# Block products: the prologue and the group steps in another order, and the probabilities scaled on ScalarE

## The chip, the cores and the metric

The kernel runs on one core of a Trainium2 chip. What counts is the device time of one execution in microseconds (us), the median over several runs. All tensors are 32-bit floats.

## The reference

Two decoder layers over 528 tokens (16 learned meta tokens ahead of 512), 1024 channels, inner width 2048. Layer 0 is gated linear attention with 4 heads, layer 1 forgetting attention with 16 heads of width 128. The change lies in layer 1:

```python
k, v, f_logit = split(rmsnorm(h, kv_norm_g) @ w_kv)            # keys and values of 16 heads, one forget logit a head
cum = cumsum(log_sigmoid(f_logit + b_forget))
q, r = split(rmsnorm(h, norm_g) @ w_in)                        # queries and gates
for start, end in blocks:                                      # 16 meta tokens, then blocks of 128
    s = q[start:end] @ k[:end].T * 128 ** -0.5 + cum[start:end, None] - cum[None, :end]
    p = softmax(where(causal, s, -1e30))
    outs.append(p @ v[:end])
h = h + (concat(outs) * silu(r)) @ w_out
out = rmsnorm(h, final_norm_g)[16:]
```

## The kernel before

Every float32 product is made of three: each operand is split into a high and a low half (a rounded copy by ScalarE, the difference by VectorE), and TensorE adds high times high, high times low and low times high (`project`, L1801). Activations lie with channels on the 128 partitions and tokens along the free dimension. Weights come in chunks of 128x1024 that SyncE loads into a ring of 6 (`raw`); ScalarE writes `w_hi` (ring of 4, L592), VectorE `w_lo` (ring of 6, L1085). The order of chunks is `CHUNKS` (L162), the order of TensorE's jobs `JOBS` (L129). Nothing is scheduled by a planner: each engine executes its own list in order, and semaphores tie them. `split_to(name)` makes all splits up to that chunk.

Layer 0 ends at 461 us. In the prologue of layer 1 TensorE makes the forget logits (`LOWF`), values of the meta tokens (m0), the keys k0, the values of the first four heads (u0, chunks u00 to u03, L2081) and the queries q0. Meanwhile VectorE takes the reciprocal root of the norm (L1104, 3.45 us), adds up the parts of the forget logits (L1588 to L1592), normalises in two halves (`norm`, L1576) and prepares keys and sums. `fox_values(0)` waits for the added logits (L2086), since its banks held their parts.

Then follows the loop over heads h (L1638 VectorE, L961 ScalarE, L2220 TensorE). Heads 2 to 11 (`strassen`, L99) make queries and gates together by seven block products on weights and on sums of tokens; their chunks are r, q and e, where e holds sums of weights made in place by VectorE (`weight_sums`, L1442). The sums of tokens (`t_raw`, `t_hi`, `t_lo`) are made once, around head 0. In such a step TensorE runs: scores of h, keys of h+1, first three products of h+1, transposes of the probabilities of h, middle three products, attention of h, last product. VectorE: maxima (L1533), low half of the first sum, the scaling of the probabilities (L1543), the keys with their norm (L1425), split of q, low keys, split of e, low probabilities, output sums. ScalarE: softmax (L896), gate by SiLU (L904), split of e, copy of the first product (L859), high keys (L842), high probabilities (L914). The scaling:

```python
nc.vector.reciprocal(inv[:, b:b + 1], tot[:, b:b + 1]).then_inc(inv_made, 1)
dve.wait_ge(inv_made, n)
v = pr[b][:, 0:KEYS[b]]
nc.vector.tensor_scalar(v, v, inv[:, b:b + 1], None, ALU.mult).then_inc(prob_scaled, 1)
```

for four blocks of 144, 272, 400 and 528 keys. Before the transposes TensorE waits for all four (L2136), before the middle products for the split of e (L2209), before the first products of head 2 for the gate of head 1 (L2199: `pe.wait_ge(fsilu_made, h)`). After heads 3, 7 and 11 stands a group step that makes the values of the next four heads (22.4 us of TensorE).

Of the kernel before, what the change touches and what calls it, by code (L numbers as in the profile page):

```python
# [11 lines left out]
P = 128  # L12
# [95 lines left out]
def fox_step(h):  # L108

    group = fox_group(h)  # L110
    jobs = [] if strassen(h) else [f"r{h}"]
# [8 lines left out]
def fox_chunks(h):  # L120
    group = fox_group(h)
    chunks = [] if strassen(h) else [f"r{h}"]
    if h + 1 < FOX_HEADS:
# [6 lines left out]
        + ["LOWF", "m0", "k0", "u0", "q0"] + [j for h in range(FOX_HEADS) for j in fox_step(h)] + [f"w{d}" for d in range(KT)])  # L130
# [4 lines left out]
for _job in JOBS:  # L135
# [19 lines left out]
    else:  # L155
# [7 lines left out]
          + ["k0", "u00", "u01", "u02", "u03", "q0"] + [x for h in range(FOX_HEADS) for x in fox_chunks(h)]  # L163
# [34 lines left out]
def program(nc, xT, consts, vecs, w_low, w_up, w_all, w_f, out, rows_out):  # L198
    with ExitStack() as c:
# [158 lines left out]
        def end_groups(g):  # L358
            if g in (0, NBLK - 1):
                return [y[0:META, (12 if g else 8) + n, 0:VH * P] for n in range(4)]  # L360
            return [ends[0:META, n // 2, n % 2 * VH * P:(n % 2 + 1) * VH * P] for n in range(4)]
# [123 lines left out]
        def _(sp):  # L485
# [37 lines left out]
            spread.update({CHUNK[f"k{h}"] + LO_RING: h for h in range(1, FOX_HEADS)})  # L523
# [55 lines left out]
        def _(act):  # L579
# [323 lines left out]

            def fox_gate(h):  # L904
# [9 lines left out]
            def probs_hi(h):  # L914
# [3 lines left out]
                if h // VH in (1, 2) and h % VH == 0:  # L918
                    act.wait_ge(end_lo, h // VH + 1)
# [34 lines left out]
            split_to("u03")  # L954
            end_values_hi(0)
            split_to("q0")
            split_to("r0")
            split_to("k1")
            fox_values_hi(0)
            queries_hi(0)  # L960
            for h in range(H):  # L961
                g = fox_group(h)
                if h + 1 < H and strassen(h + 1):
                    n = h + 1
                    split_to(f"r{n}")
                    if n == S0 or fox_group(h - 1) is not None:
                        sum_hi_first(n)
                    split_to(f"q{n}")
                    softmax(h)
                    fox_gate(h)  # L970
# [11 lines left out]
                    else:  # L982
# [7 lines left out]
                        split_to(f"r{n + 1}")  # L990
                        fox_values_hi(g)
                    continue
                if strassen(h):
                    split_to(f"q{h + 1}")
                else:
# [3 lines left out]
                softmax(h)  # L999
                if g is not None:  # L1000
                    split_to(f"u{g}0")
                elif h + 1 < H:
# [9 lines left out]
                if h == 0:  # L1012
                    for n in range(4):
                        act.wait_ge(t_made, 4)
                        nc.scalar.activation(t_hi[:, n], t_raw[:, n], ACT.Copy).then_inc(thi_made, 1)
# [5 lines left out]
                if h + 1 < H:  # L1021
# [3 lines left out]
                    else:  # L1025
                        split_to(CHUNKS[CHUNK[f"q{h + 1}"] + AHEAD])
                    queries_hi(h + 1)
                if g is not None:
# [48 lines left out]
        def _(dve):  # L1077
# [334 lines left out]
            nc.vector.memset(a_hi[0:R_ALL, AF_AT[NBLK]:AF_ALL].bitcast(F32), 0.0).then_inc(stack_zeroed, 1)  # L1412
# [988 lines left out]
```

## Time and profile before

| | us |
|---|---|
| median of 3 runs | 1028.55 (1028.09 to 1029.09) |
| the profiled execution | 1027.92, its span 1026.1 |
| TensorE busy | 1004.5 (98%) |
| VectorE busy | 692.1 (67%) |
| ScalarE busy | 534.2 (52%) |
| granted TensorE clock, mean | 0.993 |

In the views below PE is TensorE, PEld its weight loads, DVE VectorE, ACT ScalarE, POOL GpSimd, SPq the queue of SyncE. L1085 is line 1085 of the kernel. Times of a timeline are us from the start of the span, groups carry their mean in ns. What stands in brackets or behind the bar is the idle time before an instruction and what ended it. Matmuls overlap, so a start is the surer number.

### The profile page before, as it was taken

How to read it: one execution, taken by the hardware profiler on the slowest of the kernel's cores; microseconds unless marked ns; L12 is line 12 of the kernel's file. 1: busy time of each engine (PE TensorE's matmuls, PEld its weight loads, DVE VectorE, ACT ScalarE, POOL GpSimd, SP SyncE). 2: the span in 40 equal slices, each digit the busy share in tenths (PEclk: the TensorE clock that was granted, in tenths of full speed). 3: DMA queues.
4: the chain of work that ended last, by engine and by line, in shares of the span. 5: the costliest groups of instructions: out<-in, count | busy, mean ns of one | idle time of the engine just before them, and what ended most of it. 6: DMA issues, size and time to landing. Idle time of an engine off the chain costs nothing.

```text
span 1026.1 us, 18711 instructions
## 1 busy us (share of the span) xinstructions
PE 1004.5 (98%) x7627; PEld 937.6 (91%) x7627; DVE 692.1 (67%) x1142; ACT 534.2 (52%) x894; POOL 40.4 (4%) x69
## 2 busy tenths in 40 slices
PE   9999999999999999997989999999999999999998
PEld 8999999999999999995779988999899888888887
DVE  6875666677567783437779975898499846576333
ACT  6754644653483653335554654656366626464332
POOL 0000000000000000000201000100000100000000
PEclk9999999999999999998989999999999999999999
DMA  8211221121121123331323441443234553333412
GB/s 286 84 63 63 83 84 63 63 83 64 65 100 63 63 88 109 124 114 43 117 70 100 120 141 52 130 107 133 95 105 104 162 183 111 101 90 97 152 59 83
DMA packets 39798, 102.93 MB, mean 100 GB/s; under 512 B 4496, under 2 KB 12560, under 8 KB 39712
## 3 DMA queue, kind: packets, MB, share of 16 engines
q1 hardware_dynamic: 38992, 101.06, 32.1%
q8 instruction: 60, 0.98, 0.4%
q10 hardware_dynamic: 720, 0.68, 0.2%
q14 instruction: 26, 0.21, 0.1%
HBM read 94.41 MB, written 7.11 MB: 99 GB/s over the span
## 4 chain that ended last, share of the span: by engine, by line
PE 95%; DVE 2%; ACT 1%; DMA 0%; issue 0%; SPq 0%; DVEq 0%; ACTq 0%
PE psum L1808 60%; PE psum L2182 10%; PE psum L2102 9%; PE psum L2160 3%; PE psum L1933 2%; PE psum L2141 2%; PE psum L1881 1%; PE psum L2128 1%; PE psum L2129 1%; PE psum L2130 1%; PE psum L1929 1%; PE psum L1902 1%; PE psum L2067 1%; PE psum L1861 1%; DVE w_lo L1085 0%; DMA hT<-xT 0%
## 5 line engine op out<-in xcount | busy, mean ns | idle before, releaser
L1085 DVE TENSOR_TENSOR w_lo<-raw,w_hi 128x1024 fp32r<-128x1024 f32 x153 | 185.3, 1223 | 36.8 <-ACT w_hi L592 29.0
L592 ACT ACTIVATE w_hi<-raw 128x1024 fp32r<-128x1024 f32 x153 | 159.5, 1052 | 20.4 <-PE psum L2102 16.3
L1808 PE MATMUL psum<-xh,w_hi 128*128 128x264 f32 x768 | 159.1, 288 | 1.0 <-DVE w_lo L1099 0.8
L1808 PE MATMUL psum<-xl,w_hi 128*128 128x264 f32 x768 | 155.9, 285 | 0.0
L1808 PE MATMUL psum<-xh,w_lo 128*128 128x264 f32 x768 | 155.2, 283 | 0.0
L1808 PEld LDWEIGHTS psum<-xh,w_hi 128*128 128x128 f32 x768 | 118.5, 189 | 2.4 <-DVE xl L1114 1.4
L1808 PEld LDWEIGHTS psum<-xl,w_hi 128*128 128x128 f32 x768 | 119.5, 188 | 0.0
L1808 PEld LDWEIGHTS psum<-xh,w_lo 128*128 128x128 f32 x768 | 119.1, 189 | 0.0
L1808 PE MATMUL psum<-y_lo,w_hi 128*128 128x264 f32 (+2 forms) x400 | 104.8, 314 | 0.0
L571 POOL TENSOR_TENSOR sub<-sub,cst 128x128 f32<-128x128 f32 x64 | 38.7, 607 | 873.1 <-DMA sub<-sums 873.1
L1808 PEld LDWEIGHTS psum<-y_lo,w_hi 128*128 128x128 f32 x400 | 66.7, 188 | 4.6
L1099 DVE TENSOR_TENSOR hT<-psum,hT 128x528 f32<-128x528 f32 (+2 forms) x17 | 11.3, 667 | 71.1 <-PE psum L1808 71.1
L2102 PE MATMUL psum<-w_hi,zh 128*128 128x512 f32 x128 | 51.8, 405 | 6.0 <-DVE y L1099 6.0
L902 ACT ACTIVATE pr<-pr,top 128x144 f32<-128x144 f32 (+1 forms) x64 | 36.6, 573 | 32.7 <-DVE top L1531 32.7
L1808 PE MATMUL psum<-zh,w_hi 128*128 128x264 f32 x256 | 52.4, 286 | 0.8 <-DVE w_lo L1085 0.8
L1808 PE MATMUL psum<-z_hi,w_hi 128*128 128x512 f32 (+1 forms) x144 | 53.1, 369 | 0.0
L1808 PE MATMUL psum<-z_hi,w_lo 128*128 128x512 f32 (+1 forms) x144 | 52.8, 367 | 0.0
L1808 PE MATMUL psum<-y_hi,w_hi 128*128 128x264 f32 x256 | 52.0, 284 | 0.0
L1808 PE MATMUL psum<-zl,w_hi 128*128 128x264 f32 x256 | 51.9, 285 | 0.0
L1808 PE MATMUL psum<-y_hi,w_lo 128*128 128x264 f32 x256 | 51.8, 284 | 0.0
L1808 PE MATMUL psum<-zh,w_lo 128*128 128x264 f32 x256 | 51.8, 283 | 0.0
L2102 PE MATMUL psum<-w_lo,zh 128*128 128x512 f32 x128 | 51.2, 400 | 0.0
(322 smaller groups left out, 2347.0 us busy)
## 6 DMA issues: line engine op xcount, KB each, us to landing
raw<-w_all SPq DMA_DIRECT2D x143, 512.0 KB, 3.4
sub<-sums SPq DMA_DIRECT2D x16, 264.0 KB, 7.6
sub<-sums SPq DMA_DIRECT2D x16, 200.0 KB, 6.5
y_keep<-sq SPq DMA_DIRECT2D x11, 256.0 KB, 2.2
y<-y_keep SPq DMA_DIRECT2D x11, 256.0 KB, 4.0
sub<-sums SPq DMA_DIRECT2D x16, 136.0 KB, 5.0
hT<-xT SPq DMA_DIRECT2D x8, 264.0 KB, 5.4
h_keep<-hT SPq DMA_DIRECT2D x8, 256.0 KB, 4.1
```

The source lines that it names most:

```text
L571: nc.gpsimd.tensor_tensor(diag, diag, above, ALU.add).then_inc(sub_made, 1)
L592: nc.scalar.activation(w_hi[:, n % HI_RING, :], raw[:, n % LO_RING, :], ACT.Copy).then_inc(hi_made, 1)
L902: nc.scalar.activation(v, v, ACT.Exp, scale=-1.0, bias=top[:, b:b + 1], accum_out=tot[:, b:b + 1]).then_inc(prob_made, 1)
L1085: nc.vector.tensor_tensor(w_lo[:, n % LO_RING, :], raw[:, n % LO_RING, :], w_hi[:, n % HI_RING, :].bitcast(F32), ALU.subtract).then_inc(lo ...
L1099: nc.vector.tensor_tensor(out, a, b, op).then_inc(made, 1)
L1808: i = nc.tensor.matmul(o, w[a][:, k % KT, :], x[b][:, k, c0:c1], start=k == first and a == b == 0, stop=k == last and a == 1)
L1861: i = nc.tensor.transpose(bank(x + 1, b * P, (b + 1) * P), src[:, b * P:(b + 1) * P], ident)
L1933: nc.tensor.matmul(bank(x + 1, 400 - w, 400), vs[a][:, j, :], gs[b][:, A_DIAG[j]:A_DIAG[j] + w], start=False, stop=False)
L2102: i = nc.tensor.matmul(bank(4 + b), xk[a][:, k, b * BLK:(b + 1) * BLK], w[p][:, k % 2, :], start=k == a == p == 0, stop=k == KT - 1 and a ...
L2141: nc.tensor.transpose(bank(bk, c0, c0 + BLK), pr[b][:, BLK * j:BLK * j + BLK], ident)
L2160: nc.tensor.matmul(bank(slot(job), PT_Q0[j], SEQ), vs[a][:, j, v], ps[b][:, AF_AT[j]:AF_AT[j] + w], start=j == 0 and a == b == 0, stop=False)
L2182: i = nc.tensor.matmul(o, w[a][:, k0 + k, :], x[b][:, k, :], start=k == a == b == 0, stop=k == KT // 2 - 1 and a == 1)
```

## The change

The multiplies of the probabilities by their inverse sums go from VectorE to ScalarE, between the exponentials and the gate, in all 16 heads; VectorE keeps the reciprocals. In the prologue the forget logits are added ahead of the reciprocal root, the splits u01, u02 and u03 and the normalisations interleave otherwise, k1 is made right after u0, the token sums are made before head 0, and head 0 makes q1 and r1 so that head 1 makes only k2. In the group steps before heads 5 and 9 (of the block products) the split of r, both halves of the first sum and the split of q stand ahead of the value copies.

```diff
--- before.py
+++ after.py
@@ -108,7 +108,9 @@
 def fox_step(h):
 
     group = fox_group(h)
-    jobs = [] if strassen(h) else [f"r{h}"]
+    if h == 0:
+        return ["r0", "q1", "r1", "a0"]
+    jobs = [] if h <= 1 or strassen(h) else [f"r{h}"]
     if h + 1 == FOX_HEADS:
         return jobs + [f"a{h}"]
...
@@ -160,7 +164,7 @@
     _last[_area] = _job
 
 CHUNKS = ([c for h in range(GLA_HEADS) for c in gla_strips(h)] + [f"W{d}{half}" for d in range(KT) for half in "ab"]
-          + ["k0", "u00", "u01", "u02", "u03", "q0"] + [x for h in range(FOX_HEADS) for x in fox_chunks(h)]
+          + ["k0", "u00", "u01", "u02", "u03", "k1", "q0"] + [x for h in range(FOX_HEADS) for x in fox_chunks(h)]
           + [f"w{d}{half}" for d in range(KT) for half in "ab"])
 CHUNK = {c: n for n, c in enumerate(CHUNKS)}
...
@@ -901,6 +905,12 @@
                     v = pr[b][:, 0:KEYS[b]]
                     nc.scalar.activation(v, v, ACT.Exp, scale=-1.0, bias=top[:, b:b + 1], accum_out=tot[:, b:b + 1]).then_inc(prob_made, 1)
 
+            def scale_probs(h):
+                for b in range(NBLK):
+                    act.wait_ge(inv_made, NBLK * h + b + 1)
+                    v = pr[b][:, 0:KEYS[b]]
+                    nc.scalar.activation(v, v, ACT.Copy, scale=inv[:, b:b + 1]).then_inc(prob_scaled, 1)
+
...
@@ -951,22 +961,25 @@
             nc.scalar.activation(f_t, f_t, ACT.Ln, bias=1.0).then_inc(f_act, 1)
             act.wait_ge(x2_normed, 2)
             nc.scalar.activation(x2h[:, 4:8, :], x2n[:, 4:8, :], ACT.Copy).then_inc(x2h_made, 1)
-            split_to("u03")
+            split_to("k1")
             end_values_hi(0)
-            split_to("q0")
             split_to("r0")
-            split_to("k1")
             fox_values_hi(0)
+            split_to("q1")
             queries_hi(0)
+            act.wait_ge(t_made, 4)
+            for n in range(4):
+                nc.scalar.activation(t_hi[:, n], t_raw[:, n], ACT.Copy).then_inc(thi_made, 1)
...
                 if h + 1 < H and strassen(h + 1):
                     n = h + 1
                     split_to(f"r{n}")
-                    if n == S0 or fox_group(h - 1) is not None:
+                    if n == S0:
                         sum_hi_first(n)
                     split_to(f"q{n}")
                     softmax(h)
+                    scale_probs(h)
                     fox_gate(h)
...
@@ -988,17 +1001,24 @@
                         split_to(f"u{g}3")
                         split_to(f"k{n + 1}")
                         split_to(f"r{n + 1}")
+                        sum_hi_first(n + 1)
+                        split_to(f"q{n + 1}")
                         fox_values_hi(g)
...
+                elif h == 0:
+                    split_to("r1")
...
                 softmax(h)
+                scale_probs(h)
                 if g is not None:
                     split_to(f"u{g}0")
+                elif h == 0:
+                    split_to("k2")
                 elif h + 1 < H:
...
-                if h == 0:
-                    for n in range(4):
-                        act.wait_ge(t_made, 4)
-                        nc.scalar.activation(t_hi[:, n], t_raw[:, n], ACT.Copy).then_inc(thi_made, 1)
...
+                    if h == 0:
+                        split_to("r2")
...
@@ -1410,6 +1428,13 @@
             U_ORDER = (3, 2, 0, 1)
             nc.vector.memset(fv_end[0:R_ALL, :].bitcast(F32), 0.0).then_inc(stack_zeroed, 1)
             nc.vector.memset(a_hi[0:R_ALL, AF_AT[NBLK]:AF_ALL].bitcast(F32), 0.0).then_inc(stack_zeroed, 1)
+            x = slot("LOWF")
+            dve.wait_ge(f_copied, 1)
+            tt(two(fb), halves(x, H), two(f_a), ALU.add, f_sum)
+            for n, part in enumerate((f_t, f_u)):
+                dve.wait_ge(f_copied, n + 2)
+                dve.wait_ge(f_sum, n + 1)
+                tt(fb, fb, part, ALU.add, f_sum)
             done(dve, "m0")
             split_to("u00")
             inverse("x2", rstd[:])
...
@@ -1540,16 +1565,13 @@
                 maximum(h, 2)
                 maximum(h, 3)
 
-            def scale_probs(h):
+            def probs_inverse(h):
                 for b in range(NBLK):
                     n = NBLK * h + b + 1
                     dve.wait_ge(prob_made, n)
                     if h:
                         dve.wait_ge(prob_scaled, NBLK * h)
                     nc.vector.reciprocal(inv[:, b:b + 1], tot[:, b:b + 1]).then_inc(inv_made, 1)
-                    dve.wait_ge(inv_made, n)
-                    v = pr[b][:, 0:KEYS[b]]
-                    nc.vector.tensor_scalar(v, v, inv[:, b:b + 1], None, ALU.mult).then_inc(prob_scaled, 1)
 
             def probs_lo(h):
...
+            def token_sums_lo(n):
+                dve.wait_ge(thi_made, n + 1)
+                tt(t_lo[:, n], t_raw[:, n], t_hi[:, n].bitcast(F32), ALU.subtract, tlo_made)
+
...
-            x = slot("LOWF")
-            dve.wait_ge(f_copied, 1)
-            tt(two(fb), halves(x, H), two(f_a), ALU.add, f_sum)
-            for n, part in enumerate((f_t, f_u)):
-                dve.wait_ge(f_copied, n + 2)
-                dve.wait_ge(f_sum, n + 1)
-                tt(fb, fb, part, ALU.add, f_sum)
+            split_to("u01")
             dve.wait_ge(f_sum, 3)
             tt(fb, fb, rstd[0:H, :], ALU.mult, f_logit)
+            fox_key(0)
             norm(0)
-            split_to("u01")
             dve.wait_ge(f_logit, 1)
             dve.wait_ge(f_act, 1)
             nc.vector.tensor_scalar(fb, fb, vec[0:H, B_F:B_F + 1], 0.0, ALU.add, ALU.min).then_inc(f_min, 1)
+            split_to("u02")
             norm(1)
-            keys_lo(0)
-            for b in range(NBLK - 1):
-                nc.vector.memset(pr[b][:, KEYS[b]:PR_W[b]], 0.0).then_inc(pads, 1)
             dve.wait_ge(f_act, 3)
             dve.wait_ge(f_min, 1)
             tt(f_t, fb, f_t, ALU.subtract, f_log)
             dve.wait_ge(f_log, 1)
             nc.vector.tensor_tensor_scan(fb, ones[0:H, 0:1].to_broadcast([H, T]), f_t, 0.0, ALU.mult, ALU.add).then_inc(f_cum, 1)
+            split_to("u03")
             x = slot("m0") + 1
             dve.wait_ge(rtok_done, 1)
             nc.vector.tensor_copy(rtok[:, 0:NBLK], bank(x, ROOT_AT, ROOT_AT + NBLK * 32).rearrange("p (b n) -> p b n", n=32)[:, :, 0]).then_inc(rtok_made, 1)
             nc.vector.tensor_copy(rtok[0:META, NBLK:NBLK + 1], bank(x, ROOT_AT + 128, ROOT_AT + 129, 0, META)).then_inc(rtok_made, 1)
-            split_to("u02")
+            split_to("k1")
             norm_lo(0)
             end_values_sum(0)
+            norm_lo(1)
+            split_to("q0")
+            keys_lo(0)
+            for b in range(NBLK - 1):
+                nc.vector.memset(pr[b][:, KEYS[b]:PR_W[b]], 0.0).then_inc(pads, 1)
             dve.wait_ge(cum_done, 1)
             nc.vector.tensor_copy(cum_t[:].rearrange("p b h -> p (b h)"), bank(x, CUM_AT, CUM_AT + NBLK * H)).then_inc(cum_made, 1)
-            split_to("u03")
-            norm_lo(1)
             dve.wait_ge(rtok_made, 4)
             end_values_lo(0)
-            split_to("q0")
+            fox_values_lo(0)
             split_to("r0")
-            fox_values_lo(0)
+            token_sums(False)
             queries_lo(0)
...
+            token_sums(True)
+            split_to("q1")
...
@@ -1644,12 +1669,11 @@
                         split_to(f"r{n}")
                     maxima(h)
                     split_to(f"r{n}")
-                    sum_lo_first(n)
+                    if n == S0 or fox_group(h - 1) is None:
+                        sum_lo_first(n)
                     if h + 1 == S0:
-                        for i in range(4):
-                            dve.wait_ge(thi_made, i + 1)
-                            tt(t_lo[:, i], t_raw[:, i], t_hi[:, i].bitcast(F32), ALU.subtract, tlo_made)
-                    scale_probs(h)
+                        token_sums_lo(3)
+                    probs_inverse(h)
                     fox_key(n)
                     split_to(f"q{n}")
                     keys_lo(n)
@@ -1675,6 +1699,9 @@
                         split_to(f"u{g}3")
                         weight_sums(h + 2)
                         split_to(f"k{n + 1}")
+                        split_to(f"r{n + 1}")
+                        sum_lo_first(n + 1)
+                        split_to(f"q{n + 1}")
                         fox_values_lo(g)
                     continue
...
+                elif h == 0:
+                    split_to("r1")
...
-                scale_probs(h)
+                probs_inverse(h)
...
+                    if h == 0:
+                        split_to("k2")
+                    elif g is None:
                         split_to(CHUNKS[CHUNK[f"k{h + 1}"] + AHEAD])
                     fox_key(h + 1)
                     keys_lo(h + 1)
+                    if h == 0:
+                        for i in range(3):
+                            token_sums_lo(i)
...
-                    if g == 0 and part == 2:
+                    if g == 0 and part == 3:
                         sums_by_token()
...
             fox_values(0)
+            strip("k1", xk)
             pe.wait_ge(x2l_made, 2)
             strip_late("q0", xq)
...
+                elif h == 1:
+                    fox_scores(1)
+                    strip("k2", xk)
...
-                    if h + 1 < H:
+                    if h == 0:
+                        strip_late("q1", xq)
+                    elif h + 1 < H:
                         strip(f"k{h + 1}", xk)
...
                 if h + 1 < H:
-                    strip_late(f"q{h + 1}", xq)
+                    strip_late(f"q{h + 1}" if h else "r1", xq)
```

## Rows read from the trace of the kernel before

**Rows 1.** The page, busy time of each engine: us, share of the span, instructions.
```profile
PE 1004.5 (98%) x7627; PEld 937.6 (91%) x7627; DVE 692.1 (67%) x1142; ACT 534.2 (52%) x894; POOL 40.4 (4%) x69
```

**Rows 2.** TensorE's waits: who waited for whom, us in total, times, longest.
```profile
PE psum L2102 <- DVE y L1099: 6.0, 1, 6.0
PE psum L2128 <- DVE sq L1099: 5.1, 1, 5.1
PE psum L2182 <- DVE w_lo L1085: 2.6, 2, 1.3
PE psum L1808 <- DVE w_lo L1085: 0.8, 1, 0.8
```

**Rows 3.** Stretches: busy us by engine, then granted clock, DMA share, GB/s.
```profile
474.00:476.00 2.00, 2.00 (x6) 1.57 (x5) 2.00 (x2) 0.49 (x1) 0.00 (x0) 0.50 0.00 0
...
534.00:536.00 2.00, 2.00 (x8) 2.00 (x9) 1.93 (x4) 1.44 (x2) 0.00 (x0) 0.50 0.35 131
...
642.00:644.00 2.00, 0.95 (x10) 0.66 (x8) 1.76 (x3) 2.00 (x4) 0.67 (x2) 1.00 0.77 144
```

**Rows 4.** Timeline of VectorE, 466 to 475: start us, us, operation, idle before.
```profile
466.15 3.45 DVE L1104 RECIPROCAL rstd<-sq 128x528 f32<-128x528 f32 x1
...
471.04 1.50 DVE L1099 TENSOR_TENSOR y<-y 16x528 f32<-16x528 f32 x2
...
473.20 2.27 DVE L1099 TENSOR_TENSOR y<-x2g,rstd 128x2048 f32<-128x2048 f32 x1
```

**Rows 5.** Timeline of VectorE, head 1: weight sums, low halves of t, reciprocal.
```profile
533.70 0.68 DVE L1452 TENSOR_TENSOR s_raw<-raw 128x512 f32<-128x512 f32 x1
...
541.63 4.62 DVE L1099 TENSOR_TENSOR y_lo<-y,y_lo 128x1024 fp32r<-128x1024 f32 x4
...
546.18 0.16 DVE L1549 RECIPROCAL inv<-tot 128x1 f32<-128x1 f32 x1
```

**Rows 6.** ScalarE's groups, 540 to 930: busy us, mean ns, idle before.
```profile
L902 ACT ACTIVATE pr<-pr,top 128x528 f32<-128x528 f32 x15 | 10.8, 722 | 0.0
...
L902 ACT ACTIVATE pr<-pr,top 128x400 f32<-128x400 f32 x15 | 9.5, 630 | 8.0 <-DVE top L1531 8.0
...
L902 ACT ACTIVATE pr<-pr,top 128x272 f32<-128x272 f32 x14 | 7.3, 524 | 5.2 <-DVE top L1531 5.2
...
L894 ACT ACTIVATE fv_hi<-psum,rtok 128x512 fp32r<-128x512 f32 x12 | 7.3, 690 | 30.2 <-PE psum L2102 30.2
...
L902 ACT ACTIVATE pr<-pr,top 128x144 f32<-128x144 f32 x14 | 5.8, 416 | 17.6 <-DVE top L1531 17.6
...
L852 ACT ACTIVATE fq_hi<-psum 128x512 fp32r<-128x512 f32 x4 | 2.4, 598 | 9.7 <-PE psum L1808 9.7
```

**Rows 7.** Timeline of ScalarE, head 5, 659 to 664.
```profile
659.33 0.72 ACT L902 ACTIVATE pr<-pr,top 128x528 f32<-128x528 f32 x1
659.96 0.19 ACT L902 ACTIVATION_READ_ACCUMULATOR pr<-pr,top 128x1 f32 x1
660.16 1.28 ACT L907 ACT_TABLE_LOAD   x1
...
663.21 0.63 ACT L846 ACTIVATE fk_hi<-acc 128x528 fp32r<-128x528 f32 x1
```

**Rows 8.** Timeline of VectorE, head 5, 661 to 666.
```profile
661.39 0.49 DVE L1552 TENSOR_SCALAR pr<-pr,inv 128x528 f32<-128x528 f32 x1
...
663.87 0.71 DVE L1099 TENSOR_TENSOR fk_lo<-acc,fk_hi 128x528 fp32r<-128x528 f32 x1 [0.24 <-ACT fk_hi L846]
664.50 1.22 DVE L1085 TENSOR_TENSOR w_lo<-raw,w_hi 128x1024 fp32r<-128x1024 f32 x1
```

**Rows 9.** Chain that ended last, 600 to 680: start us, us, what.
```profile
644.24 4.58 PE psum L2182 x36
...
654.35 5.84 PE psum L1808 x48
```

**Rows 10.** Timeline of TensorE: first middle product of head 6.
```profile
665.85 0.50 PE L2182 MATMUL psum<-y_lo,w_hi 128*128 128x256 f32 x2
```

## What the change will do to the time

> **What bounds the kernel now.** I read the page's table of engines first: TensorE is busy 98% of the span, so what counts is where it stands still and where its clock is down [rows 1]. Then its own waits: 6.0 us before the first group of values, 0.8 us for a weight split in the second strip, 5.1 us before the scores of head 1, and 1.3 us in each of the two heads that follow a group step [rows 2]. After each of the two long waits the granted clock is at 0.50, the 1.2 GHz level, after the 1.3 us wait it stays at 1.00 [rows 3]. All the rest of the span TensorE runs without a gap. So an edit can win at most those waits with their slow stretches, about 18 us, and it can lose wherever another engine delivers only just in time. The place to look for that is the step of a block-product head (2 to 11), in the timelines of ScalarE and VectorE.
>
> There the row to see is the last split of a step. VectorE writes the low half of chunk e from 664.50 to 665.72 [rows 8], and TensorE starts the products that read it at 665.85 [rows 10]: some 0.1 us of slack. In front of it VectorE had idled 0.24 us for the high half of the keys [rows 8], which ScalarE makes as the last link of exponentials, table load, SiLU, split of e, copy, keys: the last exponential is read out at 660.15, the keys start at 663.21 [rows 7]. So ScalarE's chain sets the split of e, and the split of e sets TensorE. The pattern is the same in seven steps (heads 2, 3, 5, 6, 7, 9, 10, slack 0.05 to 0.15 us); in heads 4 and 8 it is already late by 1.3 us, the row of 644.24 being the late start [rows 9].
>
> **Part 1: the multiply on ScalarE, in all 16 heads.** VectorE loses four multiplies a head, ScalarE gains four Copies with a per-partition scale, placed between the last exponential and the table load for SiLU. No trace row shows that operation on these tiles. Nearest are the exponentials of the same four shapes, in place, with one per-partition operand: 416, 524, 630 and 722 ns [rows 6]. Consecutive ones overlap by some 0.1 us (the 528-wide one starts at 659.33 and its follower at 659.96, 0.63 us for 0.72) [rows 7], so the four hold the engine 2.29 - 0.4 = 1.9 us. Low bound: a 512-wide Copy with a scale takes 690 ns, one without 598 [rows 6]; were the operand free, 1.9 - 0.37 = 1.5 us. High bound: 2.1 us if each also pays some 0.05 us for its wait. I take 1.9, since both nearest rows with an operand agree. The four reciprocals that VectorE makes are ready before ScalarE needs the last, so they add nothing.
>
> What is queued behind: table load, SiLU, split of e, copy and keys on ScalarE all go 1.9 us later, VectorE's low keys and its split of e behind them, and TensorE waits 1.9 - 0.1 = 1.8 us more in each of the seven steps: 12.6 us. VectorE's freed time (some 1.3 us) buys nothing, since it lies behind the exponentials and becomes a wait for the keys. Nor is it caught up: VectorE's chain of a step starts at the end of the fourth product on TensorE, which moves along, so each step pays again.
>
> **Part 2: group steps.** Moving the split of r, the first sum's halves and the split of q of heads 5 and 9 ahead of the value copies takes about 2.9 us from VectorE's chain in heads 4 and 8 and 1.6 us from ScalarE's. These run in idle time there. The maxima can then follow the scores at once: last maximum about 636.5, exponentials about 637.5, scaled at 639.4, and then the 3.7 us from exponential to finished keys as in [rows 7], 0.6 and 1.2 us on VectorE [rows 8]: split of e ready near 645.0 against 644.2 today. So the gain is used up and each costs 0.7 us: 1.4 us. From head 11 on the multiplies finish early or the strip of keys covers them: nothing.
>
> **Part 3: the prologue.** Today the first values wait for three 16-row additions that stand behind a reciprocal of 3.45 us [rows 4]. With the additions ahead of it (two take 1.50 [rows 4]) the sum is ready near 466.3, the split of u00 ends near 467.5, and TensorE idles 0.9 us for 6.0, with no slow stretch. The old losses up to the first product are 6.0 + 2.0 (slow clock) + 0.8 + 5.1 + 1.9 (slow clock) = 15.8 us. Walking the new order with the durations of the old one, 2.27 for a normalisation half [rows 4], 1.2 for a split [rows 8], 5.84 for a strip of keys [rows 9], 1.28 for a table load [rows 7], I get new gaps. u02 now follows the table of f: +0.8. u03 and the root copies follow the second normalisation, which waits behind u02: +1.4. ScalarE's four t copies (3.9) now precede the softmax of head 0, and the scaled copies end 1.0 after the strip of q1. The strip of r1 reuses the bank of r0 and waits for SiLU of r0, which stands behind scaling, a split and a table load: +1.3. Three low halves of t (1.15 each, from 4.62 for four [rows 5]) stand ahead of the low probabilities: +1.3 before the attention of head 0. The scores of head 1 have no r1 part in front of them any more: +0.8.
>
> The largest is in head 1. The first product waits for SiLU of head 1 (its bank was r1's). Let X be the end of head 0's output. VectorE does weight sums, maxima, split, one low sum, one low half of t, first reciprocal: today 533.70 to 546.18, 12.5 us with four low halves [rows 5], so 9.0 with one, plus 0.1. Then ScalarE scales (1.9 + 0.1), loads the table (1.3), does SiLU (0.6) [rows 6, 7]: X + 13.0. TensorE has only scores (1.9) and the strip k2 (5.84): X + 7.7. That is a gap of 5.3 us, as long as the one it replaces, and I expect the clock to fall as it did there [rows 3]: +1.9. New losses: 0.9 + 0.8 + 1.4 + 1.0 + 1.3 + 1.3 + 0.8 + 5.3 + 1.9 = 14.7. Against 15.8 the prologue wins 1.1 us. Loads: SP's order moves k1 ahead of q0 and r0 and the sums of head 1 one slot back, to behind the maxima of head 0 and some 15 us ahead of their reader; I cost it at nothing, and if a load came late it would be one DMA of about 3.4 us.
>
> **Sum.** +12.6 + 1.4 - 1.1 = +12.9 us on the profiled execution's 1027.9 us (span 1026.1), 1040.8; the median of the runs is 0.6 above that execution, within the error. I take 1040.5.
>
> **Rivals.** (a) *The copies are hidden.* If keys and split of e had room the multiply would cost nothing, VectorE, the busier of the two, would be relieved, the 2.6 us in heads 4 and 8 would go, and the prologue would win up to 9 if the head-1 gap did not open: 1028 - 2.6 - 1.1 to - 9 = 1016 to 1024. For it: VectorE is busy some 18.5 of 20 us in these steps, ScalarE 12.5. Against it: the slack of 0.1 us and the 0.24 us wait for ScalarE [rows 8]. Chance 0.12. (b) *The clock falls at the repeated waits.* Nine waits of 1.8 to 2.0 us are longer than the 1.3 us after which it stayed up and shorter than the 5.1 us after which it fell [rows 3]. If it fell each time, at the 1.9 us taken above: 1040.5 + 9 x 1.9 = 1057.6. Chance 0.05. The Trainium skill, TensorE: Matmul & The Clock Gate, section on HAM oscillation, says that frequent short idles between groups of matmuls can let the clock swing; by that rule this case is the one to expect, and this trace shows the swing only after the two long waits. (c) *The costs and gains cancel*: scaling at 1.5 us (7 x 1.4 + 2 x 0.3 = 10.4) and a prologue that wins its full 9 us, 1029.5. Chance 0.03. Forecast (ScalarE's chain becomes the bound): 0.80.
>
> **How the numbers follow.** Own range of the forecast: low, 10.4 from scaling less up to 8 from the prologue, 1030.5; high, scaling at 2.1 (7 x 2.0 + 2 x 0.9 = 15.8) with a prologue that loses 2, 1045.7, and one or two falls of the clock, 1047. It leaves out (a), most of (b) and (c), about 0.2 in all, so 1030 to 1047 is also the range. A measurement of this kernel can tell about 0.2%, 2 us, from no change. Faster: (a), 0.12, and 0.01 of the forecast's low edge. Same: (c), 0.03. Slower: 0.84.
>
> **What would show it.** Right: TensorE waits of about 1.8 us before the middle products in seven heads and about 2.0 in heads 4 and 8, with VectorE waiting some 3.4 us for the high keys each time (0.24 + 1.9 + 1.3); the first wait of 6.0 down to about 1; a gap of some 5 us before the first product of head 2, released by SiLU. Part 1 is wrong if TensorE has no gap there, that is if the table load starts within 0.3 us of the last exponential or the keys start less than 3.5 us after it. Part 3 is wrong if the first product of head 2 starts earlier than 542 or later than 546.

## The result, and the profile of the changed kernel

The changed kernel takes 1047.38 us (median of 4 runs, 1043.55 to 1048.93); the kernel before, beside it, 1028.82 us (4 runs, 1028.09 to 1029.56). The ratio is 1.0175, 95% interval 1.0144 to 1.0205. The execution that was profiled took 1043.55 us with a span of 1041.7 us, the shortest of the four, 3.8 us under the median; why the runs differ by 5 us is a finding of its own below.

First the page of the changed kernel: span, and busy time of each engine with its share and its instructions.

```profile
span 1041.7 us, 18711 instructions
...
PE 1005.9 (97%) x7627; PEld 938.8 (90%) x7627; DVE 669.9 (64%) x1078; ACT 563.3 (54%) x958; POOL 41.4 (4%) x69
```

Against [rows 1], VectorE has 64 instructions and 22 us less, ScalarE 64 more and 29 us more, TensorE the same 7627 products. The busier helper was relieved and the kernel became longer, so the averages do not tell what happened. TensorE's waits do (who waited for whom, us in total, times, longest us), in the changed kernel:

```profile
PE psum L2215 <- DVE w_lo L1103: 18.2, 9, 2.4
PE psum L2215 <- ACT sq L922: 5.0, 1, 5.0
PE psum L1840 <- ACT sq L922: 1.2, 1, 1.2
PE psum L2134 <- DVE w_lo L1103: 1.1, 2, 0.9
PE psum L2109 <- DVE rtok L1643: 1.1, 1, 1.1
...
PE psum L2174 <- ACT pr L912: 1.0, 1, 1.0
PE psum L2193 <- DVE a_lo L1117: 0.9, 1, 0.9
PE psum L2161 <- DVE sq L1117: 0.9, 1, 0.9
```

The line number moved: L2215 is L2182 of before, and L1103 is L1085. The first row is the middle products of a step waiting for the split of e: 2 waits and 2.6 us in [rows 2], now 9 waits and 18.2 us. The second is the first product of head 2 waiting for SiLU of head 1, which was not there. The 6.0 and 5.1 us of [rows 2] are gone; the waits of about 1 us that took their place are the other rows.

The step of head 5 on ScalarE, where [rows 7] stood (start us, us, operation, shapes):

```profile
664.44 0.72 ACT L906 ACTIVATE pr<-pr,top 128x528 f32<-128x528 f32 x1
665.07 0.18 ACT L906 ACTIVATION_READ_ACCUMULATOR pr<-pr,top 128x1 f32 x1
665.16 1.96 ACT L912 ACTIVATE pr<-pr,inv 128x144 f32<-128x144 f32 x4
667.14 1.28 ACT L917 ACT_TABLE_LOAD   x1
...
670.19 0.63 ACT L850 ACTIVATE fk_hi<-acc 128x528 fp32r<-128x528 f32 x1
```

The four copies stand between the readout of the last exponential (665.07) and the table load (667.14). They hold the engine for 1.98 us, and the keys start 5.12 us after that readout begins where in [rows 7] they started 3.25 us after it. VectorE in the same step, with the idle time before an instruction and its releaser in brackets:

```profile
664.91 0.55 DVE L1574 RECIPROCAL inv<-tot 128x1 f32<-128x1 f32 x4
665.50 0.71 DVE L1450 SCALAR_TENSOR_TENSOR acc<-psum,rstd 128x528 f32<-128x528 f32 x1
...
670.85 0.92 DVE L1117 TENSOR_TENSOR fk_lo<-acc,fk_hi 128x528 fp32r<-128x528 f32 x1 [3.51 <-ACT fk_hi L850]
671.69 1.21 DVE L1103 TENSOR_TENSOR w_lo<-raw,w_hi 128x1024 fp32r<-128x1024 f32 x1
```

The time that VectorE gained stands in the brackets: 0.24 us of idle before the low keys in [rows 8], 3.51 us now. The split of e ends at 672.90, and TensorE starts the products that read it 0.06 us later, after a wait of 1.93 us:

```profile
672.96 0.51 PE L2215 MATMUL psum<-y_lo,w_hi 128*128 128x256 f32 x2 [1.93 <-DVE w_lo L1103]
```

Read one after another, the three views give the chain from a ScalarE copy to a TensorE wait, which the page's busy shares hide.

### The profile page after: what moved, and what is told of

It reads as the page before. It is cut to its first block, busy times and chain, and to the rows that moved or that the text cites. A ratio compares the mean times of both kernels' runs of the same rounds, so it can differ in the third digit from the quotient of the medians.

```text
span 1041.7 us, 18711 instructions
## 1 busy us (share of the span) xinstructions
PE 1005.9 (97%) x7627; PEld 938.8 (90%) x7627; DVE 669.9 (64%) x1078; ACT 563.3 (54%) x958; POOL 41.4 (4%) x69
## 4 chain that ended last, share of the span: by engine, by line
PE 79%; DVE 9%; ACT 7%; issue 4%; DMA 0%; DVEq 0%; ACTq 0%
PE psum L1840 54%; PE psum L2134 7%; PE psum L2215 6%; PE psum L1965 2%; PE psum L2193 2%; DVE w_lo L1103 2%; ACT pr L906 1%; PE psum L1913 1%; ACT pr L912 1%; ACT w_hi L596 1%; DVE pr L1549 1%; PE psum L1961 1%; ACT L917 1%; PE psum L2174 1%; PE psum L1934 1%
## 5 line engine op out<-in xcount | busy, mean ns | idle before, releaser
L1103 DVE TENSOR_TENSOR w_lo<-raw,w_hi 128x1024 fp32r<-128x1024 f32 x153 | 185.9, 1226 | 51.0 <-ACT w_hi L596 48.5
L1840 PEld LDWEIGHTS psum<-y_lo,w_hi 128*128 128x128 f32 x400 | 66.7, 188 | 4.6
L2215 PE MATMUL psum<-y_lo,w_hi 128*128 128x256 f32 x240 | 46.0, 293 | 18.2 <-DVE w_lo L1103 18.2
L1117 DVE TENSOR_TENSOR hT<-psum,hT 128x528 f32<-128x528 f32 (+2 forms) x17 | 11.3, 667 | 70.7 <-PE psum L1840 70.7
L2215 PEld LDWEIGHTS psum<-y_lo,w_hi 128*128 128x128 f32 x240 | 38.5, 198 | 19.4 <-DVE w_lo L1103 19.4
```

What stands on the lines that cost most here:

```text
L1103: nc.vector.tensor_tensor(w_lo[:, n % LO_RING, :], raw[:, n % LO_RING, :], w_hi[:, n % HI_RING, :].bitcast(F32), ALU.subtract).then_inc(lo ...
L1117: nc.vector.tensor_tensor(out, a, b, op).then_inc(made, 1)
L1840: i = nc.tensor.matmul(o, w[a][:, k % KT, :], x[b][:, k, c0:c1], start=k == first and a == b == 0, stop=k == last and a == 1)
L2215: i = nc.tensor.matmul(o, w[a][:, k0 + k, :], x[b][:, k, :], start=k == a == b == 0, stop=k == KT // 2 - 1 and a == 1)
```

## The experiments

All kernels compute everything. L numbers in a profile row are those of that kernel. Two theories were to be told apart. Theory A is the forecast: ScalarE's chain of exponentials, copies, table load, SiLU, split of e and keys sets TensorE in the steps, and the new order as such gains a little. Its rival B: the new order (or the extra work of the prologue) is what costs, and the copies are mostly hidden.

### One part alone, from both sides

The changed kernel with the multiplies back on VectorE (both calls of `scale_probs` go):

```
-                    scale_probs(h)
...
     nc.vector.reciprocal(inv[:, b:b + 1], tot[:, b:b + 1]).then_inc(inv_made, 1)
+    dve.wait_ge(inv_made, n)
+    v = pr[b][:, 0:KEYS[b]]
+    nc.vector.tensor_scalar(v, v, inv[:, b:b + 1], None, ALU.mult).then_inc(prob_scaled, 1)
```

> The changed kernel with the four multiplies a head back on VectorE, behind each reciprocal as in the kernel before; the new order stays. Theory (ScalarE's chain is what costs): no wait of TensorE before the middle products of the seven ordinary heads, about 0.1 us in heads 4 and 8 (1.3 before, 2.4 after); the gap before head 2's first product shrinks from 5.0 to about 1.4 us with no fall of the clock. 1027.9 - 8.9 (prologue) - 2.4 = about 1017 us. Rival (the new order costs a part of the loss): TensorE waits remain in the steps and the time is 1035 us or more.

Measured: 1017.75 us (1017.47 to 1017.95), ratio 0.9889, interval 0.9874 to 0.9903. Its TensorE waits:

```profile
PE psum L2216 <- DVE w_lo L1101: 1.3, 3, 0.6
PE psum L2194 <- DVE a_lo L1115: 1.2, 1, 1.2
...
PE psum L2216 <- ACT sq L922: 0.9, 1, 0.9
```

The new order alone wins 11.4 us. The nine waits of 18.2 us are three of 1.3 us, and the head-1 gap of 5.0 us is 0.9 us. So the copies also made the head-1 gap, and B falls: it needed a kernel that stays slow without them.

The other half, the multiplies on ScalarE in the order of before (the reverse of the diff above, in the kernel before):

```
                     softmax(h)
+                    scale_probs(h)
                     fox_gate(h)
...
-    nc.vector.tensor_scalar(v, v, inv[:, b:b + 1], None, ALU.mult).then_inc(prob_scaled, 1)
```

> The kernel before with nothing changed but the multiplies on ScalarE, between softmax and gate. Theory: seven waits of 1.8 us, 3.2 us in heads 4 and 8 (1.3 + 1.9), some 2.5 us new before head 2's first product: 1027.9 + 12.6 + 3.8 + 2.5 = about 1047 us, more if the clock falls at the new waits. Rival (the loss is the order's): within 3 us of the kernel before.

Measured: 1057.71 us (1055.94 to 1058.9), ratio 1.0281, interval 1.0264 to 1.0298, some 11 us above what was expected without falls of the clock. Its TensorE waits, then stretches of 2 us behind four of them (us from, us to, length, busy us of PE, PEld, DVE, ACT and POOL, granted clock, DMA share, GB/s):

```profile
PE psum L2187 <- DVE w_lo L1093: 22.2, 10, 3.4
PE psum L2107 <- DVE y L1107: 6.0, 1, 6.0
PE psum L2133 <- DVE sq L1107: 5.5, 1, 5.5
```

```profile
605.00:607.00 2.00, 1.75 (x8) 1.75 (x9) 1.94 (x5) 2.00 (x3) 0.45 (x1) 0.50 0.53 217
656.00:658.00 2.00, 1.95 (x9) 1.95 (x10) 1.90 (x4) 0.72 (x3) 0.31 (x1) 0.55 0.05 10
779.00:781.00 2.00, 2.00 (x12) 2.00 (x11) 1.73 (x5) 0.00 (x0) 0.00 (x0) 0.52 0.02 8
803.00:805.00 2.00, 2.00 (x10) 2.00 (x11) 1.71 (x4) 0.59 (x2) 0.58 (x2) 0.50 0.53 216
```

By the ratios the copies cost 28.9 us in the order of before and 29.4 us in the new one (1.0175 over 0.9889): the same within the intervals. In the order of before the waits explain some 20 us of it. The rest is the second thing to see here: behind four step waits of 1.7 to 3.4 us (heads 3, 4, 8 and 9) the granted clock is at 0.50 to 0.55, the 1.2 GHz level. The sum of 1 minus the granted clock over stretches of 1 us, called the lost clock below, is 14.6 us in this kernel and 7.0 us in the one before; each of the four falls has 1.7 us of it.

### How much slack the chain has

A small dose: 0.6 us of idle copies on ScalarE, into unused memory, in the same place of the kernel before.

```
                     softmax(h)
+                    for v in (spare[:, 0:106], spare[:, 106:212], spare2[:, 0:106]):
+                        nc.scalar.activation(v, reset[:, 0:106], ACT.Copy)
                     fox_gate(h)
```

> The kernel before with three idle copies of 106 columns on ScalarE between softmax and gate of heads 1 to 10, into unused memory, some 0.6 us. Theory (0.1 us of slack, each us on ScalarE there is a us of TensorE): waits of 0.5 us in seven heads and 1.9 in heads 4 and 8: 1027.9 + 3.5 + 1.2 = about 1032.6. Rival (ScalarE has room, only moving the multiplies as such costs): no change, 1028.

Measured: 1034.83 us (1034.76 to 1034.95), ratio 1.0055, interval 1.004 to 1.007. The waits for the split of e:

```profile
PE psum L2184 <- DVE w_lo L1087: 6.5, 9, 1.8
```

By time these are 0.48, 0.39, 1.82, 0.40, 0.39, 0.40, 1.83, 0.39 and 0.40 us in heads 2 to 10. The idle copies put off the table load of head 5 by 0.54 us: it starts 0.74 us behind the start of the last readout (662.98), where in [rows 7] it starts 0.20 us behind it.

```profile
662.98 0.19 ACT L902 ACTIVATION_READ_ACCUMULATOR pr<-pr,top 128x1 f32 x1
...
663.72 1.28 ACT L907 ACT_TABLE_LOAD   x1
```

So work that only takes ScalarE's time, with nothing of the probabilities in it, comes out on TensorE less some 0.1 us in six of the seven steps (0.54 to 0.4), and whole in heads 4 and 8, from 1.3 to 1.8. The slack of 0.1 us that the forecast read from [rows 8, 10] is thus shown. Behind both 1.8 us waits the clock fell (granted 0.72 and 0.73 in the 2 us behind), 1.7 us of lost clock each; the fall of head 1, ahead of them, is 1.7 us where the kernel before has 3.4. The lost clock is 8.8 us against 7.0, and these 1.8 us are most of the 2.2 us by which the run is above the expectation.

### Taking the link out

If it is the chain, its table load and SiLU can be moved out of it while the copies stay. In the changed kernel, the gate of heads 2 to 10 behind the high halves of the probabilities:

```
                     scale_probs(h)
-                    fox_gate(h)
+                    if h < S0:
+                        fox_gate(h)
                     split_to(f"e{n}")
...
                     probs_hi(h)
+                    if h >= S0:
+                        fox_gate(h)
```

> The changed kernel with the gate (table load and SiLU, 1.9 us) of heads 2 to 10 moved behind the high probabilities on ScalarE; the multiplies stay there. Theory (a serial chain exponentials, copies, gate, split of e, keys): the chain is as long as in the kernel before again, the seven waits vanish (-13), those of heads 4 and 8 fall to about 0.1 (-4.6), with them the fall of the clock in head 2 (-1.8): about 1024 us. The prologue keeps its 5 us gap. Rival (ScalarE is too busy, or the copies slow something else): the waits stay and the time is 1040 or more.

Measured: 1025.31 us (1024.9 to 1025.52), ratio 0.9962, interval 0.9947 to 0.9977. Its TensorE waits, and ScalarE in head 5:

```profile
PE psum L2218 <- ACT sq L922: 5.0, 1, 5.0
...
PE psum L2218 <- DVE w_lo L1106: 0.7, 2, 0.4
```

```profile
657.83 1.97 ACT L912 ACTIVATE pr<-pr,inv 128x144 f32<-128x144 f32 x4
659.70 1.04 ACT L596 ACTIVATE w_hi<-raw 128x1024 fp32r<-128x1024 f32 x1
...
665.64 1.28 ACT L917 ACT_TABLE_LOAD   x1
666.94 0.63 ACT L917 ACTIVATE sq<-sq 128x512 f32<-128x512 f32 x1
668.80 0.63 ACT L861 ACTIVATE fq_hi<-acc 128x512 fp32r<-128x512 f32 x1 [1.23 <-DVE acc L1120]
```

The 1.9 us of load and SiLU took the place that the copies had filled, seven waits are gone and the two of heads 4 and 8 are 0.41 and 0.34 us. The gate is not missed at its new place: ScalarE still idles 1.23 us behind it. The changed kernel is 22 us shorter with the same copies when the split of e stands right behind them; 17.5 us of that are the waits, the rest was not traced and goes with the clock (0.993 to 0.995, where the changed kernel had 0.989 to 0.994).

The head-1 gap in the same manner, alone:

```
                     softmax(h)
+                    if h == 1:
+                        fox_gate(h)
                     scale_probs(h)
-                    fox_gate(h)
+                    if h > 1:
+                        fox_gate(h)
```

> The changed kernel with head 1's gate ahead of its scaling on ScalarE, all else kept. Theory (head 2's first product waits for the SiLU of head 1, which stands behind the reciprocals and the copies): the wait falls from 5.0 to about 0.8 us, the fall of the clock behind it goes (-1.9): 5.8 us less than the changed kernel, its profiled execution would be at 1037.7. Rival (that wait covers another, for the low halves of t or the scaled probabilities): less than 2 us gained.

Measured: 1037.84 us (1037.24 to 1039.27), ratio 1.0082, interval 1.0066 to 1.0098. The rows of its waits:

```profile
PE psum L2218 <- DVE w_lo L1106: 18.1, 9, 2.4
...
PE psum L2218 <- ACT sq L922: 0.9, 1, 0.9
```

The 5.0 us are 0.9 us and the nine step waits stay. The time fell by 9.5 us, where the theory had 5.8. The waits account for 4.2 of it, and the rest goes with the clock: the changed kernel ran at a mean granted clock of 0.986 to 0.996, this one at 0.996 to 0.998, though nine waits of the same length stand in it. Its profile has a fall behind the waits of heads 2 and 3 only, 1.7 us of lost clock each. Why fewer falls follow the same waits here is not shown. In the changed kernel SiLU of head 1 stood behind copies that began only when VectorE had made the reciprocals, and that wait (2.11 us in the first row) was in the gap too:

```profile
540.08 1.97 ACT L912 ACTIVATE pr<-pr,inv 128x144 f32<-128x144 f32 x4 [2.11 <-DVE inv L1574]
542.07 1.28 ACT L922 ACT_TABLE_LOAD   x1
543.36 0.60 ACT L922 ACTIVATE sq<-psum 128x512 f32<-128x512 f32 x1
```

Both moves together, copies on ScalarE:

```
                     softmax(h)
+                    if h == 1:
+                        fox_gate(h)
                     scale_probs(h)
-                    fox_gate(h)
...
                     probs_hi(h)
+                    if h >= S0:
+                        fox_gate(h)
```

> The changed kernel, multiplies on ScalarE, with head 1's gate ahead of its scaling and the gates of heads 2 to 10 behind the high probabilities. Theory: both repairs add up: 1025.3 - 5.8 = 1019.5 us, perhaps 1.6 less if the fall of the clock at 520 us doesn't come. That is 2 us above the multiplies on VectorE with the new order alone (1017.8), from the gaps of head 0. Rival (moving the multiplies pays once the chain is short): 1016 or less.

Measured: 1019.3 us (1018.86 to 1019.39), ratio 0.9899, interval 0.9884 to 0.9914. The theory had 1019.5, and its rival, that the copies pay once the chain is short, had 1016 or less. With both links out, the copies cost 3.0 us (against the kernel below that has the multiplies on VectorE and late gates, 1016.34 us) instead of 29. So rival (a), copies hidden, describes an order of work that this kernel could have had, not the one it has.

### The group steps alone

The kernel before with only the hoist behind the strips of a group step:

```
-                    if n == S0 or fox_group(h - 1) is not None:
+                    if n == S0:
                         sum_hi_first(n)
...
                         split_to(f"r{n + 1}")
+                        sum_hi_first(n + 1)
+                        split_to(f"q{n + 1}")
                         fox_values_hi(g)
```

and the same three steps on VectorE ahead of the low value halves.

> The kernel before with only the order of the group steps changed (split of r, halves of the first sum and split of q of heads 5 and 9 ahead of the value copies). Theory: in heads 4 and 8 the wait of 1.3 us falls to about 0.6, what stays is ScalarE's chain behind the maxima, as in the run with all of the new order and the multiplies on VectorE (0.5 and 0.6): 1028.9 - 1.5 = 1027.4 us, 0.15% less. Rival (the moved splits come too late for the value products, or wait for their ring slots): new waits in the group steps, 1029 or more.

Measured: 1027.4 us (1025.79 to 1029.38) against 1029.09 us, ratio 0.9981, interval 0.9971 to 0.9991. The waits for the split of e:

```profile
PE psum L2188 <- DVE w_lo L1087: 0.9, 3, 0.4
```

The 1.3 us of heads 4 and 8 are 0.38 and 0.39, which is 1.8 us, and 1.7 us came (0.9 to 3.0 by the interval). Taken from the 11.4 us that the new order wins, that leaves nearly 10 us for the prologue; this is a difference, the prologue was not run by itself.

### The best of both

The first experiment's kernel with the gates of heads 2 to 10 late, as in the experiment that took the gate out of the chain. The lines show ScalarE's part against the changed kernel; on VectorE the multiplies stand behind the reciprocals as in the first experiment.

```
                     softmax(h)
-                    scale_probs(h)
-                    fox_gate(h)
+                    if h < S0:
+                        fox_gate(h)
...
                     probs_hi(h)
+                    if h >= S0:
+                        fox_gate(h)
```

> The new order with the multiplies on VectorE and in addition the gate of heads 2 to 10 behind the high probabilities on ScalarE. Theory: takes 1.9 us off ScalarE's chain, the last waits in the steps (0.5, 0.6 and 0.2 us) go: 1017.8 - 1.3 = 1016.5 us. Rival (VectorE itself is the bound there, or the late gate delays the outputs and the scores of the next head): the same or slower than 1017.8.

Measured: 1016.34 us (1015.75 to 1016.58), ratio 0.9871, interval 0.9854 to 0.9888, the shortest of all: 13.3 us under the kernel before by the ratio, and 31 us under the changed one. It takes the new order and not the copies.

### The changed kernel again

Its runs lay 5 us apart, so it was run once more as it is, for another profile.

> The changed kernel once more, unchanged, for a second trace. Theory (its executions differ by where the clock falls at the ten waits): the waits stand at the same places with the same lengths within 0.2 us, the time is about 1036 us plus the time lost to the lower clock, so about 1037 at a mean clock of 0.997 and 1048 at 0.989, and the trace shows falls after other waits than the one in head 2. Rival (something else varies, a DMA or a wait): the waits differ, and times differ at the same mean clock.

Measured: 1047.04 us (1042.66 to 1050.4, 5 runs), ratio 1.0156, interval 1.0131 to 1.0181; this time the profiled execution is a long one, span 1048.6 us at a mean granted clock of 0.986, against 1041.7 us at 0.994. The waits for the split of e and for SiLU are the same:

```profile
PE psum L2215 <- DVE w_lo L1103: 18.1, 9, 2.5
PE psum L2215 <- ACT sq L922: 5.0, 1, 5.0
```

The clock is not. Stretches in the first profile of the changed kernel, behind the waits of heads 1, 2 and 7:

```profile
543.00:545.00 2.00, 0.90 (x4) 0.93 (x5) 0.00 (x0) 1.89 (x3) 0.69 (x2) 0.50 0.88 315
577.00:579.00 2.00, 2.00 (x12) 2.00 (x11) 1.20 (x3) 0.00 (x0) 0.00 (x0) 0.50 0.00 0
...
722.00:724.00 2.00, 2.00 (x19) 2.00 (x18) 1.57 (x4) 0.00 (x0) 0.00 (x0) 1.00 0.01 2
```

and in the second profile, behind those of heads 2, 7 and 8:

```profile
579.00:581.00 2.00, 2.00 (x12) 2.00 (x11) 1.52 (x4) 0.00 (x0) 0.00 (x0) 0.53 0.00 0
722.00:724.00 2.00, 1.78 (x9) 1.78 (x10) 1.94 (x5) 2.00 (x4) 0.46 (x1) 0.62 0.61 238
773.00:775.00 2.00, 2.00 (x14) 2.00 (x13) 1.90 (x5) 0.00 (x0) 0.00 (x0) 0.67 0.00 0
```

In both, 2.0 to 2.1 us of wait ahead of head 2's products was followed by the 1.2 GHz level. The 1.72 us of head 7 was followed by 1.00 in one execution and 0.62 in the other, and the 2.4 us of head 8 by a fall in the second alone. In the second profile the clock also fell after waits of 1.0 and 1.3 us near 520, and after 1.99 us near 797, but not after 1.90 us at 603, 2.46 us at 652 or 1.99 us at 822. The losses of clock sum to 5.4 us in the first profile and 14.3 us in the second; the difference of 8.9 is more than the 6.9 us between their spans. The two are not the same measure: a stretch in which TensorE idles loses nothing by its clock, and a slower TensorE can hide a later wait. The 0.92 us before the attention of head 0 in the first profile (`PE psum L2193 <- DVE a_lo L1117`) is missing in the second, where the clock had fallen just ahead of it. The other executions of the same runs were at 1040.8 us (0.994), 1041.0 (0.996), 1045.2 (0.990) and 1046.9 (0.990): the two at 0.990 are 4 to 6 us longer than the two above, though within such a pair the order does not follow the clock.

## Why the prediction was right, and where it was short

The forecast was 1040.5 us, in a range of 1030 to 1047; the profiled execution took 1043.55 and the median is 1047.38, a little over the upper edge. The forecast counts from 1028.55 us, and the ratio on that gives 1046.6, inside the range. Of the change, 12 us were forecast and 18 came: the side was right, and so was the cause, but a third of the size was missing, most of it the clock. By its steps:

- **Part 1, mechanism.** Right, by the two kernels that do one part each, by the dose and by taking the gate out of the chain. TensorE waits in just the seven heads named, and VectorE waited 3.51 us for the high keys where 3.4 was stated.
- **Part 1, size.** The four copies hold ScalarE 1.98 us, where 1.9 was taken and 2.1 was the upper bound. The nearest rows, exponentials with one operand per partition, were the right ones. ScalarE's groups of the changed kernel (busy us, mean ns, idle before):

```profile
L912 ACT ACTIVATE pr<-pr,inv 128x528 f32<-128x528 f32 x15 | 10.8, 723 | 0.0
...
L912 ACT ACTIVATE pr<-pr,inv 128x144 f32<-128x144 f32 x15 | 6.1, 406 | 3.6 <-DVE inv L1574 3.6
```

  723 ns against the exponential's 722, 406 against 416 [rows 6]. The overlap between them was overestimated: the sum of the four (723 + 616 + 508 + 406 = 2.25 us) less 1.96 leaves 0.1 us for each of three borders, not four. The seven waits are 2.07, 1.85, 1.93, 1.83, 1.72, 1.99 and 1.98 us, 13.4 together for the 12.6 of the sum. The 0.1 us a step that the sum lacks lies in part on VectorE, whose work the forecast moved later with its old durations: the low half of the keys takes 0.71 to 0.96 us in these seven steps, over 0.8 in four of them, where in the kernel before one of seven is over 0.8.
- **Part 2.** The step "0.7 us each" was short: heads 4 and 8 wait 2.44 and 2.42 us, against 1.3 each before, so 1.1 each, 2.3 us for 1.4. It implies 1.2 us won by the hoist and 1.9 lost by the copies; the group experiment shows 0.9 won, the copies take 1.98, and 1.98 - 0.9 is 1.1.
- **Part 3.** The walk was right in nearly every row. Forecast and measured: before the first values 0.9 and 0.91 us; u02 0.8 and 0.22; u03 with the root copies 1.4 and 1.08; scaled copies of head 0 1.0 and 0.99; SiLU of r0 1.3 and 1.25; low halves of t 1.3 and 0.92; scores of head 1 0.8 and 0.88; head-1 gap 5.3 and 4.99; first product of head 2 "542 to 546" and 544.10. VectorE's timeline shows the reordered additions, two of them now ahead of the reciprocal where [rows 4] had them behind it:

```profile
464.51 1.50 DVE L1117 TENSOR_TENSOR y<-y 16x528 f32<-16x528 f32 x2
465.93 1.21 DVE L1103 TENSOR_TENSOR w_lo<-raw,w_hi 128x1024 fp32r<-128x1024 f32 x1
467.07 3.43 DVE L1122 RECIPROCAL rstd<-sq 128x528 f32<-128x528 f32 x1
```

  The transposes of head 1 begin at 550.60, at 551.98 before: 1.4 us won, 1.1 forecast. That the sum came so close is in part luck. The waits ahead of that point add up to 11.9 us before and 11.2 us now, where the forecast's own rows give 11.9 and 12.8. The slow stretches were sized at 1.9 to 2.0 us each; from the same jobs at either clock they cost about 1.3 us (the first values), 1.7 us (the scores of head 1) and, in the changed kernel, 2.2 us (the first product of head 2, 6.50 us from its start to the transposes against 4.29). That leaves a gain of 1.5 us, 0.3 more than the prologue shows, for 0.2 us of the 1.4 were there ahead of the first of these waits; what the 0.3 us are was not traced. The products just ahead of that wait start at 464.65 where they started at 464.87.
- **What was missing.** The clock. The forecast let it fall once in the changed kernel, after the head-1 gap, and gave its fall at the repeated waits a chance of 0.05, as a fall at all nine. The truth is between: it falls at some, another set in each execution. In the first profile it is one more fall, 1.7 us of lost clock in head 2; in the second there are six falls in all, and its span is 6.9 us longer. The term that was mis-sized is the clock's at the nine waits. The sum has nothing for it, although the forecast itself says that its rows leave open what happens between 1.3 us and 5.1 us; it gave a price to none or to all, and only its upper bound has "one or two falls". Its row for the 1.3 us wait is also taken too early, from 642 to 644, before the wait has ended at 644.24. The stretch behind the wait, in the kernel before, says the same:

```profile
644.00:646.00 2.00, 1.76 (x14) 1.76 (x15) 1.94 (x5) 0.94 (x4) 0.96 (x2) 1.00 0.78 297
```

  The Trainium skill, TensorE: Matmul & The Clock Gate, section A second HAM failure mode: psum-queue depth-cycling, was cited by the forecast (as the section on HAM oscillation) for falls at frequent short idles. The two profiles of the changed kernel agree with it as far as short idles bring falls, after 1.7 to 2.5 us in some places and none in others.
- **Rivals.** (a), copies hidden, is wrong here for the reason given against it, the slack of 0.1 us; (c) needed the prologue's full gain, which the head-1 gap took away, also by the copies: without them it is there, 1017.75 us.

Profiled spans add up so: seven steps 13.4, heads 4 and 8 2.3, prologue -1.4, the fall in head 2 1.7, in all 16.0 us, for the 15.6 us from 1026.1 to 1041.7. The 3.8 us from the profiled execution to the median go with the clock in its sister executions (spans of 1046.8 us at 0.989, 1047.1 at 0.989, 1044.4 at 0.993); where it fell in them no trace shows.

## What to carry to other kernels

Compare two engines by the slack of the chain that ends in the bottleneck's wait, not by their busy shares: 2 us of work a head, moved from an engine at 67% to one at 52%, cost 29 us here, because it went in front of a table load on the one chain with 0.1 us to spare. When an operation must go onto such a chain, first look for another that can leave it: with the gate of head 1 ahead of the copies and the later gates behind the probabilities, the same copies cost 3 us. A repeated wait of 2 us on TensorE is to be priced higher than its length, and with a spread, since the clock may fall behind any of them.

## What the runs showed that was not expected

- The granted clock fell to the 1.2 GHz level after waits of 1.0 and 1.3 us near each other (in the second profile of the changed kernel and in the one with the gate late, but in three other profiles with the same pair it did not), and after single ones of 1.7 to 2.5 us, and it stayed up after others of 1.9 to 2.5 us in the same execution. Which waits were followed by a fall differed between two executions of one kernel (5.4 and 14.3 us of lost clock); each fall behind a step wait had 1.7 us of lost clock, also in the kernel with the copies alone. What tells the waits with a fall from those without was not settled.
- An in-place copy with a per-partition scale costs ScalarE what an exponential of the same shape does (723 and 722 ns at 528 columns), 0.72 us where VectorE's multiply took 0.49 [rows 8].
